# Four edits to a two-block transformer kernel: the place of the normalized stream in SBUF, the order of splits around two latent chains, and the first loads

## What is computed

```python
u = _rmsnorm(h, mix_pre_g[l])                  # mixer of layer l, l = 0, 1
proj = u @ w_in[l]                             # values, queries, keys, memory queries
g = sigmoid(u @ w_gate[l] + b_gate[l])         # 3 x 1024 gates

# latent attention
ckv = rms_norm(h, kv_in_norm) @ w_dkv          # key latent (256) and rotated key (64)
kv = rms_norm(ckv[..., :256], kv_norm) @ w_ukv # 8 heads of keys (128) and values (128)
q = rms_norm(x_n @ w_dq, q_norm) @ w_uq        # 8 heads of 128 + 64 rotated
p = softmax(mask((q_nope @ k_nope.T + q_rope @ k_rope.T) * scale))
o = (p @ v) @ w_o
```

## Time and profile before

| | |
|---|---|
| median of 3 runs | 1854.07 us (1853.8 to 1854.56) |
| profiled execution | 1853.9 us |
| its span, first to last instruction | 1852.1 us |
| granted TensorE clock, mean | 0.999 |
| TensorE busy (10463 matmuls) | 99% |
| weight loads of TensorE | 87% |
| VectorE, ScalarE, GpSimd busy | 65%, 56%, 5% |
| chain that ended last | TensorE 95%, VectorE 2%, ScalarE 1%, DMA 1% |
| read from HBM | 331 MB, 179 GB/s over the span |

### The profile page before, as it was taken

One profiled execution on the slowest core, in us unless ns is written; L12 is line 12 of the kernel. 1 busy time (PEld: TensorE's weight loads), 2 busy tenths in 40 slices (PEclk: granted clock), 3 DMA queues, 4 the chain that ended last, 5 costly groups with the idle time before them and its releaser, 6 DMA issues.

```text
span 1852.1 us, 26991 instructions
## 1 busy us (share of the span) xinstructions
PE 1835.9 (99%) x10463; PEld 1619.9 (87%) x10463; DVE 1211.2 (65%) x1824; ACT 1033.8 (56%) x1680; POOL 97.4 (5%) x78
## 2 busy tenths in 40 slices
PE   8999999999999999999999999999999999999998
PEld 7888899998888888888999888888889998889997
DVE  5555657787765466545777786555768765768763
ACT  6445554555654455445555655444557654757653
POOL 0000001110000000000011100000002210001210
PEclk9999999999999999999999999999999999999999
DMA  8655575445576547554654547654747665537652
GB/s 271 211 183 181 168 207 158 144 151 178 177 224 189 188 148 231 184 193 132 194 176 149 182 147 231 191 184 147 225 139 216 185 196 157 177 103 203 197 192 103
DMA packets 353792, 333.83 MB, mean 180 GB/s; under 512 B 25338, under 2 KB 299392, under 8 KB 353664
## 3 DMA queue, kind: packets, MB, share of 16 engines
q1 hardware_dynamic: 353088, 331.57, 58.3%
q10 hardware_dynamic: 576, 0.53, 0.1%
HBM read 330.97 MB, written 1.05 MB: 179 GB/s over the span
## 4 chain that ended last, share of the span: by engine, by line
PE 95%; DVE 2%; ACT 1%; DMA 1%; issue 0%; ACTq 0%; SPq 0%
PE bank L1685 22%; PE bank L1687 22%; PE bank L1686 22%; PE bank L1696 7%; PE bank L1697 7%; PE bank L1698 7%; PE bank L1702 3%; DVE wlo L1079 1%; DVE U L1127 1%; PE bank L1936 0%; PE bank L2002 0%; PE bank L1973 0%; PE bank L2007 0%; DMA raw<-in_ffn_w_up 0%; ACT junk_h L597 0%
## 5 line engine op out<-in xcount | busy, mean ns | idle before, releaser
L1079 DVE TENSOR_TENSOR wlo<-raw,whi 128x1024 fp32r<-128x1024 f32 (+3 forms) x638 | 762.1, 1202 | 436.4 <-ACT whi L558 434.8
L558 ACT ACTIVATE whi<-raw 128x1024 fp32r<-128x1024 f32 (+3 forms) x638 | 648.1, 1024 | 497.0 <-PE bank L1687 404.0
L1685 PE MATMUL bank<-whi,U 128*128 128x512 f32 (+2 forms) x1232 | 471.7, 383 | 2.8 <-DVE U L1127 1.7
L1687 PE MATMUL bank<-wlo,U 128*128 128x512 f32 (+2 forms) x1232 | 459.9, 373 | 0.0
L1686 PE MATMUL bank<-whi,U 128*128 128x512 f32 (+2 forms) x1232 | 459.4, 373 | 0.0
L1696 PE MATMUL bank<-U,whi 128*128 128x256 f32 x1024 | 290.6, 284 | 0.0
L1697 PE MATMUL bank<-U,whi 128*128 128x256 f32 x1024 | 287.8, 281 | 0.0
L1698 PE MATMUL bank<-U,wlo 128*128 128x256 f32 x1024 | 287.1, 280 | 0.0
L1685 PEld LDWEIGHTS bank<-whi,U 128*128 128x128 f32 x1232 | 231.4, 188 | 37.8 <-DVE wlo L1079 2.6
L1687 PEld LDWEIGHTS bank<-wlo,U 128*128 128x128 f32 x1232 | 231.2, 188 | 35.6
L1686 PEld LDWEIGHTS bank<-whi,U 128*128 128x128 f32 x1232 | 231.7, 188 | 32.9
(11 more groups left out here) (287 smaller groups left out, 1727.7 us busy)
## 6 DMA issues: line engine op xcount, KB each, us to landing
raw<-in_ffn_w_up SPq DMA_DIRECT2D x351, 256.0 KB, 3.5
raw<-in_ffn_w_down SPq DMA_DIRECT2D x264, 256.0 KB, 2.9
raw<-in_ffn_w_gate SPq DMA_DIRECT2D x175, 256.0 KB, 2.9
raw<-in_w_gate SPq DMA_DIRECT2D x128, 192.0 KB, 3.0
raw<-in_w_in SPq DMA_DIRECT2D x80, 256.0 KB, 3.5
raw<-in_a_w_in SPq DMA_DIRECT2D x48, 256.0 KB, 3.1
raw<-in_w_mem_kv SPq DMA_DIRECT2D x32, 256.0 KB, 3.3
raw<-in_w_out SPq DMA_DIRECT2D x32, 256.0 KB, 3.1
```

The source lines that it names most:

```text
L558: act.activation(whi[n % SLOTS][:, 0:w], raw[n % RAW][:, 0:w], ACT.Copy).then_inc(hi_ready, 1)
L1079: dve.tensor_tensor(wlo[n % SLOTS][:, 0:w], raw[n % RAW][:, 0:w], whi[n % SLOTS][:, 0:w].bitcast(F32), ALU.subtract).then_inc(lo_ready, 1)
L1685: pe.matmul(dst, xh, wh, start=start, stop=False)
L1687: return pe.matmul(dst, xh, wl, start=False, stop=stop)
```

## The change

The edits are these.

- Streams 1 and 4, those of the two mixers, lie 80 columns on as streams 7 and 9 do, and the mixers' value, memory-query, feature and gate chunks read them there.
- SP waits for the first half of x before it issues chunk 1; the first two fills of turns on TensorE have 8 and 2 turns instead of 12 and 4.
- In the mixer, VectorE makes `rb` ahead of `split_to(n0 + 1 + SLOTS)` instead of after it.
- In the latent attention, ScalarE takes the squares of the key latent ahead of c_hp to c_hp+2 instead of after them, and later splits up to c_hp+1 and c_hp+3 where it did up to c_hp+3 and c_hp+5.
- VectorE normalizes the key latent ahead of those chunks too, handles c_hp before the rotation of the key and c_hp+1 after it, and turns the first half of the queries before the low parts of the key latent.
- `mla_pT` of heads 0 and 1 comes ahead of the exponentials of heads 2 and 3, and that of heads 2 and 3 ahead of those of heads 4 and 5.

```diff
-        conv_hi, conv_lo = ucols(80), ucols(KT * TOK + 80)
-        stream_hi = lambda b: conv_hi if b in (7, 9) else uhi
-        stream_lo = lambda b: conv_lo if b in (7, 9) else ulo
+        shifted_hi, shifted_lo = ucols(80), ucols(KT * TOK + 80)
+        stream_hi = lambda b: shifted_hi if b in (1, 4, 7, 9) else uhi
+        stream_lo = lambda b: shifted_lo if b in (1, 4, 7, 9) else ulo
...
             g0, u0 = A["ffn1_w_gate"][0], A["ffn1_w_up"][0]
+            sp.wait_ge(x_loaded[0], 16)
             load(1, both(g0, u0, 2, 0))
...
-            split_to(c_hp + 2)
             act.wait_ge(lat0_full, 2)
             latent_square(1, 0, bank[6][:, 0:KVL], stat(8, 0, RSTD))
...
             act.preload_act_table(ACT.Exp)
-            split_to(c_hp + 3)
+            split_to(c_hp + 1)
             act.wait_ge(qr0_full, 1)
...
                                scale=par[:, KVN + k:KVN + k + 1]).then_inc(lat_hi, 1)
-            split_to(c_hp + 5)
+            split_to(c_hp + 3)
...
             split_to(c_hp + 4 + SLOTS)
+            heads(0, mla_pT)
             mla_exp(2)
             take_key(2)
             mla_exp(3)
             take_value(2)
-            heads(0, mla_pT)
             split_to(c_hp + 5 + SLOTS)
...
             heads(0, mla_high)
+            heads(1, mla_pT)
             mla_exp(4)
             mla_exp(5)
-            heads(1, mla_pT)
...
                 b, n0 = 3 * l + 1, c_v[l]
-                split_to(n0 + 1 + SLOTS)
                 for t in range(TT):
                     dve.wait_ge(rstd_done, 2 * b + t + 1)
                     dve.tensor_scalar(rb[:, t, :], ones, stat(b, t, RSTD), None, ALU.mult).then_inc(rb_done, 1)
+                split_to(n0 + 1 + SLOTS)
                 split_to(n0 + 11 + SLOTS)
...
-            split_to(c_hp + 2)
             for t in range(TT):
                 latent(1, t, bank[6 + t][:, 0:KVL], ctk[:, t, :])
+            split_to(c_hp)
             dve.wait_ge(kr_raw, 2)
...
-            split_to(c_hp + 3)
+            split_to(c_hp + 1)
...
+            turn_query(0)
             for k in range(2):
                 dve.wait_ge(lat_hi, 6)
...
-            turn_query(0)
             turn_query(1)
...
-                    return token_block(n0 + i, j, t, 0, bank[2 * (blk % 2) + t][:, 0:VB], VB, uhi, ulo,
+                    return token_block(n0 + i, j, t, 0, bank[2 * (blk % 2) + t][:, 0:VB], VB, shifted_hi, shifted_lo,
...
-                        project(bank[n % 2][:, 0:TOK], c + n, KT, uhi, ulo).then_inc(w_used, 1)
+                        project(bank[n % 2][:, 0:TOK], c + n, KT, shifted_hi, shifted_lo).then_inc(w_used, 1)
...
-                            ins = token_block(n, i, t, 0, bank[t][:, 0:GB], GB, uhi, ulo)
+                            ins = token_block(n, i, t, 0, bank[t][:, 0:GB], GB, shifted_hi, shifted_lo)
...
-            keep_busy(12)
+            keep_busy(8)
...
-            keep_busy(4)
+            keep_busy(2)
```

More of the change, by code:

```diff
@@ L1916, in mem_query @@
                     start_chunk(c_qm[l] + h)
-                    project(bank[QUERY_BANK[h]][:, 0:TOK], c_qm[l] + h, KT, uhi, ulo).then_inc(w_used, 1)
+                    project(bank[QUERY_BANK[h]][:, 0:TOK], c_qm[l] + h, KT, shifted_hi, shifted_lo).then_inc(w_used, 1)
                 if l == 0:
@@ L2132, in conv_ffn @@
                             start_chunk(n0 + j)
-                        ins = token_block(n0 + j, j, t, 0, bank[4 + t][:, :], 512, conv_hi, conv_lo, lambda k: u_ready(b, t, k))
+                        ins = token_block(n0 + j, j, t, 0, bank[4 + t][:, :], 512, shifted_hi, shifted_lo, lambda k: u_ready(b, t, k))
                         if t == 1:
@@ L2147, in conv_ffn @@
                         start_chunk(n)
-                        project(bank[conv_bank(f)][:, s * TOK:(s + 1) * TOK], n, KT, conv_hi, conv_lo).then_inc(w_used, 1)
+                        project(bank[conv_bank(f)][:, s * TOK:(s + 1) * TOK], n, KT, shifted_hi, shifted_lo).then_inc(w_used, 1)
                         if f == 2 and s == 0:
```

## The result

| | before | after |
|---|---|---|
| median of 20 runs each, same chip | 1853.78 us (1852.59 to 1855.43) | 1856.91 us (1855.64 to 1858.29) |
| ratio, 95% interval | | 1.0016 [1.0010, 1.0023] |
| span of the profiled execution | 1852.1 us | 1855.1 us |

A forecast was written before the change was run, and what follows sets the result against it. TensorE, busy 1835.9 of 1852.1 us, was taken as the bound. Shift +3.3, reciprocals -0.95, latent attention +2.25 and start 0 sum to +4.6 us: span 1856.7, forecast median 1858.7 us, range 1852.6 to 1861.0.

The forecast's parts named there:

- shift, moving: Mixer projections, stream moving: 320 bytes on shortens 960 matmuls from 119.9 to 117.8 ns each, 2.0 us gained.
- shift, standing: Mixer value and gate blocks, stream stationary: 1056 matmuls lose 5.0 ns each, 5.3 us lost (ends 0 and 6.3).
- reciprocals: Mixer in layer 1: made ahead of the splits, TensorE's wait at their turn goes, 0.95 us gained (0.6 to 0.96).
- start: Program start: the gain from x landing earlier ends at the later chunk 4; 0, ends -0.5 and +0.6 us.
- key copy behind the load of c_hp+6: Latent attention: the late load holds ScalarE's key copy, so query_heads(1) starts 3.1 us later (+2.4 to +4.3).
- clock in that wait: Latent attention: clock falls while TensorE waits 4.9 us before query_heads(1), about 2 us more; 1860.7 us, chance 0.15.
- probabilities: Latent attention: copied ahead of two exponentials, TensorE's wait at 1628.89 goes, 0.85 us gained (0.4 to 0.9).
- Rival (a): Mixers' 344- and 384-wide blocks don't feel the shift; shift is then -2.0 us, total 1853.4 us; chance 0.16.
- The sign it named: Mixer gate blocks: steps of 178 to 180 ns would show the forecast loss, clearly under 177 its absence.
- Key latent ahead: Latent attention: squares first end TensorE's key-latent wait but delay c_hp+2's split and c_hp+6's load; query_heads(1) 3.1 us later.
- Rival (d): Latent attention: clock falls to 1.2 GHz in the 4.9 us wait before query_heads(1), about 2 us more; chance 0.15.

The follow-up runs named there:

- the kernel worth keeping with the order of before: Changed kernel with the latent attention order of before except turned probabilities first, no SP wait for x, longer fill of turns: 1849.23 us, ratio 0.9974.
- 32 turns: Changed kernel with 32 identity turns on TensorE into a free bank ahead of query_heads(1): 1856.83 us, ratio 1.0016.
- the second kernel worth keeping: As the kernel worth keeping with the order of before, plus the key latent's squares and scaling ahead of the splits: 1849.23 us, ratio 0.9975.

## Why the prediction was right, and where its parts were wrong

The measured time lies in the range, and slower was the way forecast, but several terms were badly sized and cancelled each other.

| term | forecast | measured |
|---|---|---|
| shift, moving | -2.0 | -3.0 |
| shift, standing | +5.3 | +0.8 |
| reciprocals | -0.95 | -1.0 |
| start | 0 (-0.5 to +0.6) | +1.39 |
| key copy behind the load of c_hp+6 | +3.1 (2.4 to 4.3) | +4.0 |
| clock in that wait | a rival, +2 | +1.74 |
| probabilities | -0.85 | -1.11 (the same alone) |
| sum | +4.6 | +2.8 by these terms (+2.94 at the last matmuls, +3.1 by the medians) |

**Shift, moving.** The 3.0 is 960 x 3.1 ns (122.2 and 122.3 down to 119.5 and 118.8). The forecast took one unbroken stretch, 2.1 ns a step. Its mechanism held; the size was off, because the settled step is not one value: the shifted stream has its memory queries at 113.4 and at 117.8 ns, and the feature chunks, at 123.8 to 124.1 ns before, now step at 117.4 to 122.5, some gaining 6 ns and some 2.

**Shift, standing: the step that failed.** It carried a loss seen at 512 columns over to 384 and 344, at 5.0 ns per matmul. In after it is 768 x 0.7 + 288 x 1.0 = 0.8 us. With the shift alone it is 0.15 + 0.29 = 0.4 us. Rival (a) was right on this term, though its chance was set at 0.16. The argument against it, that both stages which have the loss show it throughout, was about the wide form alone. The forecast took rows of a restart for the gates (rows 5, 17.1 ns on top of the columns) and called the loss 2.5 to 6.0 ns. Their mean in the same trace, 177.8 ns, is 17.8 ns on top. If the shifted form adds 19.6 ns at every width, as the forecast assumed, that leaves 1.8 ns for a gate matmul, 1.4 us in all. The value blocks had no row: their mean, 158.0 ns with 143.3 for the 344 columns, leaves 5.0 ns, 1.4 us more. So even the forecast's own rule gave 2.8 us and not 5.3. The addition of the gates without any shift already differed from the 13.6 ns of the wide form, so it was not the same for all widths, and the value of 5.0 had no row of its own. Nor did any run move the 512-wide form: that its 6.0 ns come from the shift at all is read from two stages and not tested. The sign it named could not decide either: 178.6 ns in the gate blocks lies in its 178 to 180, but before stood at 177.8 already.

**Reciprocals.** From the last value matmul ahead of the turn to the first behind it: 1.31 us before, 0.30 after. Right in mechanism and size.

**Start.** The forecast looked at chunk 4 alone and found its load hidden. It saw that chunk 3 lands later and gave that no price: chunk 3, issued 3.2 us later, landed 2.8 us later (15.0), and ScalarE stood 2.34 us for it. The upper end of 0.6 for this term was too narrow for a queue delayed by 3.6 us.

**Key latent ahead.** In the time of before (1.71 us added, the difference with which TensorE comes into the stage), VectorE's split of c_hp+2 would be at 1597.3 (forecast 1597.4) and the load at 1598.6, as forecast; TensorE's query turns would end at 1599.4, forecast 1599.3. Off is only the landing: 4.45 us for the later half instead of the 3.6 taken, which with the split behind it is the 0.9 us by which the wait exceeds its forecast; it stays within the bounds given (4.7). The split and the key copy follow as forecast.

**Clock.** Rival (d) came about, in place and in size. The forecast had set it at 0.15 beside 0.45 for none, although its own rows (rows 13) had the fall about 4 us behind the last matmul and the wait at 4.9. Given those rows, the fall was the likelier case and should have stood in the sum. The Trainium skill, "TensorE: Matmul & The Clock Gate", "HAM oscillation", tells of kernels whose engine returns to the lower level while it waits for a DMA; the trace of after agrees, with 5.70 us idle behind a load and 0.50 granted from 1601 to 1607.

Two errors of opposite sign (shift 5.5 us too slow; start, landing and clock 4.0 too fast), and 0.3 for the probabilities and reciprocals, left 1.8 us. That the predicted time came so near is in part luck: with the shift alone sized as measured, the forecast would have been 1853.2, 3.7 us too fast.

## What to carry to other kernels

Before moving a split, follow its buffer, not its engine: the raw buffer it frees decides when a load four chunks on is issued, and whatever copy stands behind that chunk's split on another engine inherits the delay. Price an operand's place from rows of the same width and role, or run it alone; a loss seen at 512 columns said little for 384. And where a forecast opens a wait of several microseconds in front of TensorE, count the lower clock behind it as part of the price.

## What the runs showed of the hardware

- Where the moving float32 operand starts matters: 320 bytes on, 118.6 ns per 256-wide step; 0, 128 and 256 bytes on, 121.8 to 122.3. The Trainium skill, "TensorE: Matmul & The Clock Gate", "Back-to-back issue gap", has no address in its formula, which it gives for an isolated matmul; an estimate by it is about 109 ns for 256 columns. The runs show 113.4 at the least. Whether it is the odd multiple of 64 bytes that helps, and why, was not tried; the weights' own place was never moved.
- The clock can fall after TensorE has resumed. It did so 1.2 to 1.4 us after the restart behind a pause of 1.97 us (the kernel worth keeping with the order of before: lower level from about 1590.3), of 2.15 us (32 turns) and of 2.25 us (128 bytes). Behind one of 2.37 us (the split of c_hp+2 moved) it fell 0.3 us ahead of the restart. It stayed at 1.00 behind the 1.74 us of before at the place of the first, but also behind 2.21 us at the start of the second kernel worth keeping (up to 10.50), so the length of the pause alone does not tell. The stretches of the first of these:

```profile
1590.00:1591.00 1.00, 1.00 (x9) 1.00 (x8) 1.00 (x2) 1.00 (x3) 0.00 (x0) 0.65 0.83 248
1591.00:1593.00 2.00, 2.00 (x11) 2.00 (x11) 1.54 (x5) 2.00 (x4) 0.00 (x0) 0.50 0.38 124
1593.00:1594.00 1.00, 1.00 (x8) 1.00 (x7) 0.93 (x3) 0.52 (x2) 0.00 (x0) 0.64 0.90 307
```

There the 1.3 us lost were absorbed by a wait that followed (1.07 us idle in before, ahead of the rotated queries' turn), so they cost nothing in the end.
